# Another order for the layers of the first block of a two-block transformer kernel

## The chip, the cores and the metric

The kernel runs on one core of one Trainium2 chip. The metric is the device time of one execution in microseconds (us): three runs of the kernel before gave 2479.18, 2482.4 and 2484.06 us, median 2482.4. Everything is computed in float32, and the whole program is one launch.

## What is computed

A sequence of 256 tokens of width 1024 goes through two blocks, each with two layers. The change touches the first block alone. Each of its layers computes this (`hgrn2` is a gated linear recurrence, `nsa` an attention with three branches):

```
h = rmsnorm(x);  proj = h @ w_in            # 1024 x 7704, split in 13 parts
o_h = rmsnorm(hgrn2(hq, hf, hi)) * silu(hz) # 8 heads of 128
k_cmp, v_cmp = compress(kc), compress(vc)   # 15 blocks of 32 tokens, stride 16
for each of 8 heads in 2 groups:
    o_c = softmax(q k_cmp) v_cmp ; o_s = softmax(q ks) vs ; o_w = softmax(q kw) vw
    o_n = g0 * o_c + g1 * o_s + g2 * o_w    # g = sigmoid(ng), 24 columns
o_n = o_n * silu(nz)
x = x + rmsnorm([o_h, o_n] @ w_out)         # 2048 x 1024
```

The recurrence's state decays per channel and token by f; its lower bound is 0 in layer 0 and a learned one in layer 1, so layer 1 has a longer chain of elementwise work between the projection f and its first product. With four blocks of 64 keys and 16 blocks selected, the selected branch is full causal attention here. The second block (two feed-forward parts, a three-way mixing, a cross attention, twice) is not changed.

## The kernel before, in words

**Program.** `make_plan` (line 624 on) writes one list of steps by hand-written generators, and five functions (`tensor_program`, `scalar_program`, `vector_program`, `gpsimd_program`, `sync_program`) turn it into the queue of each engine. A step is issued on every engine in the order of the list, so each engine works through its parts of the steps in that order, and an instruction that waits holds everything behind it on its engine. The buffers come from two shelves, first in first out: 24 SBUF units of 128x1024 (`NUNIT`) and the 8 PSUM banks. Who takes one waits for the events with which it was given back.

**Matmuls.** A projection multiplies in three passes of fp32r: high x high, low x high and high x low. A weight piece (1 MB, 128x2048) is loaded by SyncE into one of 6 slots; ScalarE copies its high part (L1872, 1.9 us), VectorE subtracts for the low part (L2053, 2.3 us), and for each third piece GpSimd does it (L2540, 4.6 us). `split_next` lets this run at most three pieces (`LEAD`) ahead of the piece last finished. `mm_tok` gives a "wide" step: 12 matmuls of 512 columns (L1625, L1629, L1635), tokens in the partitions; a piece has one for each half t of the tokens. `mm_ch` gives a "channel" step: 12 matmuls of 256 columns (L1649, L1652, L1655), channels in the partitions.

**Interleaving.** `weave(plan, main, side, us)` takes one step of `main`, then steps of `side` until `us` microseconds' worth of matmul columns have been planned. `both` takes a step of each of several generators in turn. A `"rest"` from the side ends its turn early.

**A layer's order** (`first_layer`): (1) norm, keys and values of both branches; (2) the projection c, then `compress` beside q and the first part of nz with the gates; (3) `nsa(0)` and `nsa(1)` in turn, with the rest of nz, hv and hz beside them (`proj_all`); (4) `hgrn_qf(0)`, the projections f and q of head group 0 and their elementwise chain; (5) `hgrn_heads(0)` beside `hgrn_qf(1)`; (6) `hgrn_heads(1)` beside the output projection of the attention half; (7) the output projection of the recurrence half (`tail`).

**The parts.** An attention branch of one group and half (`nsa`) has three steps: scores (L1673, VectorE scales and masks them at L2109, takes the maximum at L2114; ScalarE the exponentials at L1920), transposes of the probabilities (L1681), and the product with the values (L1690). `nsa_out` then takes, on VectorE, the sums' inverse times the gate (L2273, L2275, L2278), and adds the scaled product of the branch to an SBUF accumulator (L2286 for the first branch, L2291 for the others). The gates are 24 columns at the head of the nz projection, so nz is cut in 6656+512, 7168+512 and 7680+24 columns, the last with 24-column matmuls. `hgrn_heads` has a product within the token (L1745), one across the halves (L1756), and seven levels: VectorE makes the key factor (L2373), GpSimd the query factor's exponent (L2564, 1.1 us), ScalarE the exponential (L2013), VectorE the query product (L2378), TensorE the level's matmuls (L1767, 16 records), and VectorE copies them under a mask (L2384). `level` is issued `depth` levels ahead: 1 for group 0, 2 for group 1. At the end `hgrn_v` (L1777, L1779) multiplies with the values. In `compress`, `cmp_rows` (L2254) lays out the rows for `cmp_1` (L1711). `tables()` computes constants of layer 1 and of the second block, and in layer 0 it is a third stream beside attention.

Of the kernel before, what the change touches and what calls it, by code (L numbers as in the profile page):

```python
# [11 lines left out]
ALU = mybir.AluOpType  # L12
# [23 lines left out]
NUNIT = 24  # L36
# [224 lines left out]
class Memory:  # L261
    def __init__(self, nc, ctx):
# [16 lines left out]
        self.halfs = sb("halfs", [P, 16])  # L279
        self.ropes = sb("ropes", [P, 2, 224])  # L280
# [10 lines left out]
def weave(plan, main, side, us):  # L291
# [20 lines left out]
def both(*gens):  # L312
    gens = list(gens)
    while gens:
        for g in list(gens):
            more = next(g, "end")
            if more == "end":
                gens.remove(g)
            else:
                yield more  # L320


class Plan:
# [208 lines left out]
    def pv(self, name, res, nh, of, vd, need):  # L532
        bank = self.B.take()
        self.work += 4 * nh * len(res) * vd
        self.do("pv", name=name, res=[(w3, made) for _, w3, made in res], nh=nh, of=of, vd=vd, need=need, bank=bank)
# [62 lines left out]
def tail(plan, seam, ws, mid=None, first=False):  # L598

    for t in range(2):  # L600
        for wi, (w, k0, h) in enumerate(ws):
            for pi, (kk0, p) in enumerate(w):
# [6 lines left out]
        if t == 0:  # L609
            if mid:  # L610
                mid()
            seam.turn(0)
# [11 lines left out]
def make_plan(A, m, order):  # L624
# [71 lines left out]

    def first_layer(l, seam):
# [19 lines left out]

        kT, vv = U.take(), U.take()
# [15 lines left out]
        cc = U.take()  # L734
        for q, (b, pr) in enumerate((yield from proj_ch(f"{N}.c", 5120, 512))):
            cc_made = plan.copy(f"{N}.cc{q}", [pr], cc.ap[:, q * 512:q * 512 + 512], b.ap, "dve", cc.after)
            B.give(b, cc_made)

        qT = [U.take(), U.take()]
# [14 lines left out]
        def q_side():  # L754
            k_turn()
# [13 lines left out]
            yield from nz_proj([(6656, 512)])  # L769
            q_turn(1, *qrows[1])  # L770

        def q_turn(g, qs, rt):
            q_made[g] = []
# [4 lines left out]
        kcm = U.take()  # L778
        kcs, vcs = kcm.ap[:, 0:32], kcm.ap[:, 64:320]
        kc_made = []  # L780

        def compress():
            for which in range(2):
# [6 lines left out]
                   need=[cc_made, ("gT",)], after=e.after)  # L790
# [27 lines left out]
                if which == 0:  # L818
# [10 lines left out]
                                  b.ap[:, 0:32].rearrange("p (g n) -> p g n", g=2)[:, :, 0:15], "dve", kcm.after)  # L829
                else:  # L830
                    c = plan.copy(f"{C}.vc", [("cmp_2", C)], vcs[0:15, :], b.ap[0:15, 0:256], "dve", kcm.after)
# [4 lines left out]
        gates = [st(24), st(24)]  # L836
        nz = [U.take(), U.take()]
        g_made, nz_made = [None, None], [[], []]

        def nz_proj(cols):  # L840
            for c0, n in cols:
                for t, (b, pr) in enumerate((yield from proj_tok(f"{N}.z{c0}", c0, n))):
                    o = 24 if c0 == 6656 else 0
                    if o:
                        do("gates", name=(N, t), need=pr, dst=gates[t], src=b.ap[:, 0:24])
                    d0 = c0 + o - 6680
                    s = plan.silu(f"{N}.nz{c0}{t}", [pr], nz[t].ap[:, d0:d0 + n - o], b.ap[:, o:n], nz[t].after)
                    B.give(b, s, *([("gates", N, t)] if o else []))
                    nz_made[t].append(s)
                if o:  # L850
                    for t in range(2):
                        do("gates_scaled", name=(N, t), ap=gates[t])
                        g_made[t] = ("gates_scaled", N, t)
                yield
# [1838 lines left out]
```

## Time and profile before

| | |
|---|---|
| median of three runs | 2482.4 us |
| profiled execution, its own time | 2484.2 us |
| its span, first to last instruction | 2482.4 us |
| TensorE matmuls busy | 2219.2 us, 89% of the span |
| TensorE weight loads (overlap) | 1941.7 us, 78% |
| VectorE, ScalarE, GpSimd busy | 1320.1, 1017.7, 567.4 us |
| mean granted TensorE clock | 0.948 of full speed |
| chain that ended last | PE 66%, DVE 17%, ACT 9%, issue 5%, POOL 3%, DMA 1% |
| HBM | 141 GB/s over the span |

PE is TensorE, DVE VectorE, ACT ScalarE, POOL GpSimd. In a row of windows the first number is the length, then for each engine its busy time and its instructions, then the granted clock of TensorE (1.00 is 2.4 GHz, 0.50 is 1.2 GHz, and a mean between them is a mixture), the share of the DMA engines and GB/s. Length less PE busy is TensorE's idle time. In a row of a timeline stand the start, the time from the first start to the last end, the engine, the line of the kernel, and in brackets how long the engine had been idle and what ended that. Where GpSimd and VectorE run at the same time, single rows can be longer than their operation. In a row of waits stand who waited for whom, the total, how many times, and the longest.

### The profile page before, as it was taken

What the parts mean: (1) busy time and instruction counts of PE and PEld (TensorE: products, weight loads), DVE (VectorE), ACT (ScalarE), POOL (GpSimd) and SP (SyncE); (2) the same over time, 40 slices, a digit from 0 to 9 for tenths busy, and PEclk for the clock granted to TensorE, in tenths of its full rate; (3) what the DMA queues carried; (4) which work ended last, traced back from release to release, by engine and by line L of the source; (5) the groups of instructions that cost most, each with busy time, mean ns of one, the idle gap of its engine ahead of it and who ended that gap; (6) DMA issues with size and microseconds to landing.
All of it is one profiled execution on the core that took longest, in us unless ns stands there. A gap on an engine that the chain in (4) does not pass through costs nothing.

```text
span 2482.4 us, 29939 instructions
## 1 busy us (share of the span) xinstructions
PE 2219.2 (89%) x12751; PEld 1941.7 (78%) x12751; DVE 1320.1 (53%) x1663; ACT 1017.7 (41%) x1340; POOL 567.4 (23%) x215
## 2 busy tenths in 40 slices
PE   6897888899877799988998999999998998898998
PEld 5786876678776689867877879988986777686997
DVE  4456564536576554356476554345435545755533
ACT  4244543334443344335444444334433445443442
POOL 1110222202023132222122323223222222222221
PEclk9988998999888999999999999999999999998999
DMA  7442212444122345524444436555553354343553
GB/s 234 140 141 80 103 68 88 142 156 138 66 76 78 102 170 187 176 102 136 158 165 140 158 110 204 187 178 171 187 188 109 117 169 169 127 158 105 191 186 108
DMA packets 190974, 351.63 MB, mean 142 GB/s; under 512 B 8124, under 2 KB 84984, under 8 KB 190840
## 3 DMA queue, kind: packets, MB, share of 16 engines
q1 hardware_dynamic: 189400, 344.46, 41.2%
q0 software_dynamic: 1440, 5.24, 0.6%
q8 instruction: 101, 1.65, 0.3%
q14 instruction: 33, 0.27, 0.0%
HBM read 348.63 MB, written 1.05 MB: 141 GB/s over the span
## 4 chain that ended last, share of the span: by engine, by line
PE 66%; DVE 17%; ACT 9%; issue 5%; POOL 3%; DMA 1%; SPq 0%; DVEq 0%; POOLq 0%; ACTq 0%
PE bank L1629 12%; PE bank L1635 12%; PE bank L1625 12%; PE bank L1655 7%; PE bank L1652 7%; PE bank L1649 7%; ACT high L1872 4%; DVE raw_r L2053 3%; PE bank L1673 2%; PE bank L1690 2%; POOL raw_r L2540 2%; PE bank L1711 1%; DVE units_r L2070 1%; DVE units L2384 1%; PE bank L1664 1%
## 5 line engine op out<-in xcount | busy, mean ns | idle before, releaser
L2540 POOL TENSOR_TENSOR raw_r<-raw,high 128x2048 fp32r<-128x2048 f32 (+2 forms) x104 | 482.9, 4644 | 1391.3 <-ACT high L1872 1391.3
L1625 PE MATMUL bank<-high,units_r 128*128 128x512 f32 (+2 forms) x1728 | 702.3, 407 | 48.5 <-ACT units_r L1889 21.8
L2053 DVE TENSOR_TENSOR raw_r<-raw,high 128x2048 fp32r<-128x2048 f32 x210 | 531.4, 2538 | 388.4 <-ACT high L1872 388.4
L1629 PE MATMUL bank<-high,units_r 128*128 128x512 f32 (+2 forms) x1728 | 688.6, 399 | 11.9 <-DVE units_r L2070 11.7
L1872 ACT ACTIVATE high<-raw 128x2048 fp32r<-128x2048 f32 (+1 forms) x314 | 589.9, 1892 | 235.3 <-PE bank L1635 189.7
L1635 PE MATMUL bank<-raw_r,units_r 128*128 128x512 f32 (+2 forms) x1728 | 467.4, 393 | 4.3 <-POOL raw_r L2540 4.3
L1625 PEld LDWEIGHTS bank<-high,units_r 128*128 128x128 f32 x1728 | 337.1, 195 | 120.5 <-issue 42.0
L1629 PEld LDWEIGHTS bank<-high,units_r 128*128 128x128 f32 x1728 | 337.2, 195 | 84.9 <-DVE units_r L2070 20.3
L1649 PE MATMUL bank<-units_r,high 128*128 128x256 f32 x1600 | 399.3, 285 | 0.0
L1652 PE MATMUL bank<-units_r,high 128*128 128x256 f32 x1600 | 396.9, 284 | 0.0
L1635 PEld LDWEIGHTS bank<-raw_r,units_r 128*128 128x128 f32 x1728 | 330.4, 193 | 75.2 <-POOL raw_r L2540 7.0
L1649 PEld LDWEIGHTS bank<-units_r,high 128*128 128x128 f32 x1600 | 309.1, 193 | 0.9
L1652 PEld LDWEIGHTS bank<-units_r,high 128*128 128x128 f32 x1600 | 308.9, 193 | 0.9
L1655 PE MATMUL bank<-units_r,raw_r 128*128 128x256 f32 x1600 | 235.1, 284 | 2.4 <-POOL raw_r L2540 2.2
L1655 PEld LDWEIGHTS bank<-units_r,raw_r 128*128 128x128 f32 x1600 | 211.5, 193 | 2.8 <-POOL raw_r L2540 2.4
L1920 ACT ACTIVATE units<-units,stat 128x256 f32<-128x256 f32 (+2 forms) x176 | 74.0, 422 | 201.6 <-DVE stat L2116 201.6
L2529 POOL TENSOR_TENSOR stat<-stat,halfs 128x1 f32<-128x1 f32 (+2 forms) x64 | 43.5, 679 | 453.0 <-DVE stat L2142 197.2
L2070 DVE TENSOR_TENSOR units_r<-units,units_r 128x512 fp32r<-128x512 f32 x100 | 81.7, 846 | 72.0 <-ACT units_r L1889 69.4
L1889 ACT ACTIVATE units_r<-units 128x512 fp32r<-128x512 f32 x100 | 61.3, 631 | 140.3 <-DVE units L2062 108.5
L2081 DVE SCALAR_TENSOR_TENSOR units<-units,bank 128x512 f32<-128x512 f32 (+2 forms) x68 | 43.5, 652 | 121.0 <-ACT units L1900 121.0
L1767 PE MATMUL bank<-units 128*128 128x128 f32 x448 | 66.0, 309 | 30.2 <-DVE units L2378 19.6
L1767 PEld LDWEIGHTS bank<-units 128*128 128x128 f32 x448 | 62.7, 222 | 34.1 <-ACT units L2013 15.5
(217 smaller groups left out, 1820.6 us busy)
## 6 DMA issues: line engine op xcount, KB each, us to landing
raw<-in_ffn_w_dram SPq DMA_DIRECT2D x132, 1024.0 KB, 5.1
raw<-in_w_in_dram SPq DMA_DIRECT2D x108, 1024.0 KB, 4.9
raw<-in_w_out_dram SPq DMA_DIRECT2D x24, 1024.0 KB, 5.0
raw<-in_cross_wkv_dram SPq DMA_DIRECT2D x16, 1024.0 KB, 5.0
raw<-in_w_branch_dram SPq DMA_DIRECT2D x12, 1024.0 KB, 4.8
raw<-in_cross_wq_dram SPq DMA_DIRECT2D x8, 1024.0 KB, 5.2
raw<-in_cross_wo_dram SPq DMA_DIRECT2D x8, 1024.0 KB, 4.9
raw<-in_w_in_dram SPq DMA_DIRECT2D x4, 832.0 KB, 4.3
```

What stands on the lines that cost most here:

```text
L1625: pe.matmul(o, h.high(k0 + k)[:, span], w[:, k, :], start=start and k == 0, stop=False, skip_group_check=True)
L1629: pe.matmul(o, h.low(k0 + k)[:, span], w[:, k, :], start=False, stop=False, skip_group_check=True)
L1635: product = pe.matmul(o, h.high(k0 + k)[:, span], w[:, k, :], start=False, stop=stop and k == p.k - 1, skip_group_check=True)
L1649: pe.matmul(o, w, h.high(k0 + k), start=first and k == 0 and c % 2 == 0, stop=False, skip_group_check=True)
L1652: pe.matmul(o, w, h.low(k0 + k), start=False, stop=False, skip_group_check=True)
L1655: product = pe.matmul(o, p.lo[:, k, c * P:c * P + P], h.high(k0 + k), start=False, stop=last and k == p.k - 1, skip_group_check=True)
L1767: score = pe.matmul(bank.ap[:, i * P:i * P + P], r3[:, i, t * P:t * P + P], r3[:, i, t * P:t * P + P], start=True, stop=True, skip_group_c ...
L1872: act.activation(high, p.raw, ACT.Copy).then_inc(*mark(s.whigh, ("whigh", p.i)))
L1920: done = act.activation(p3[:, h, :], p3[:, h, :], ACT.Exp, bias=mx[:, h:h + 1], scale=1.0, accum_out=sm[:, h:h + 1])
L2053: dve.tensor_tensor(low, p.raw, high.bitcast(F32), ALU.subtract).then_inc(*mark(s.wlow_v, ("wlow", p.i)))
L2070: dve.tensor_tensor(seen(lo.r, t), seen(lo.ap, t), seen(hi.r, t).bitcast(F32), ALU.subtract).then_inc(*mark(s.alow, ("low", name, q)))
L2540: pool.tensor_tensor(low, p.raw, high.bitcast(F32), ALU.subtract).then_inc(*mark(s.wlow_p, ("wlow", p.i)))
```

## The change

`first_layer` gets another order; the second block's code stays as it is.

- After keys and values, `hgrn_qf(0)` comes first. Then four streams run in turn through one `weave` with 2.0 us a step: `compress`, `nsa(0)`, `nsa(1)` and `recurrence` (both head groups, one after the other), in layer 0 with `tables()` as the fifth. A stream whose inputs aren't planned yet yields `"stuck"` and is passed over; where all are stuck, `weave` takes one step of the side.
- The side is `fill()`: all projections in one row (c, q, gates, hv and hz of group 0, then after the end of recurrence 0 f and q of group 1, nz in two halves, hv and hz of group 1), then, once attention is done, the output projection of head group 0 of the recurrence and of group 0 of attention (`out_early`). The `tail` has the two others.
- The gates have a projection of their own in channel form (24 rows), transposed back to tokens; nz is then 2 x 512 columns, and no 24-column matmul is left.
- The gate and the inverse of the sum are multiplied into the probabilities before they are transposed (`nsa_gate`), so that the three branches add up in one PSUM bank, held by the group and half from its first branch to `nsa_cat`.
- hv and hz are kept per head group; `depth` is 1 for both groups; the compressed keys and values lie in a buffer of their own; `NUNIT` is 26.

```diff
 def weave(plan, main, side, us=None):
...
+        if more == "stuck":
+            assert live and next(side, "end") != "end"
+            yield
+            continue
...
 def both(*gens):
     gens = list(gens)
     while gens:
+        went = False
         for g in list(gens):
             more = next(g, "end")
             if more == "end":
                 gens.remove(g)
-            else:
+                went = True
+            elif more != "stuck":
+                went = True
                 yield more
+        if not went:
+            yield "stuck"
...
+        def gate_proj():
+            ((_, p),) = plan.weight(w_in, 0, 8, 6656, 24)
+            b, u, b2 = B.take(), U.take(), B.take()
+            do("gate_rows", name=N, p=p, h=h, bank=b, dst=u)
...
+            do("gate_turn", name=N, src=u.ap, bank=b2, dst=both_gates)
...
         def nsa(g):
+            while q_made[g] is None or len(kc_made) < 2:
+                yield "stuck"
...
                     u, p3, sm, soft = plan.scores(S_, [*q_made[g], *k_need], 4, L, of, 1, bias, P ** -0.5)
                     yield
+                    do("nsa_gate", name=S_, need=[soft, g_made], sm=sm, ..., p3=p3, L=L, some=br > 0)
                     res = plan.turned(...)
                     yield
...
-                    b, pr = plan.pv(S_, res, 4, vf, P, [*v_made, *kc_made])
-                    do("nsa_out", ...)
+                    acc, pr = plan.pv(..., None if br == 0 else acc, br == 0, br == 2)
                     yield
+                while (g, t) not in nz_made:
+                    yield "stuck"
...
-            depth = 1 + hg
+            depth = 1
...
+            while ("v", hg) not in st_ or ("z", hg) not in st_:
+                yield "stuck"
...
+        def recurrence():
+            yield from hgrn_heads(0)
+            while ("qf", 1) not in st_:
+                yield "stuck"
+            yield from hgrn_heads(1)
+
+        def projections():
+            yield from cmp_proj()
+            k_turn()
+            yield from q_proj()
+            yield from hgrn_v(0)
+            yield from hgrn_z(0)
+            while ("done", 0) not in st_:
+                yield "rest"
+            yield from hgrn_qf(1)
+            yield from nz_proj(0)
+            yield from nz_proj(1)
+            yield from hgrn_v(1)
+            yield from hgrn_z(1)
...
+        def out_early():
+            while len(cat_made) < 4:
+                yield "rest"
+            for t in range(2):
+                turn_h(0, t)
+            yield from plan.mm_tok(f"{N}.oh0", plan.weight(w_out, 0, 4, 0, 1024), h_T[0], yb, last=False)
+            turn_n(0)
+            yield from plan.mm_tok(f"{N}.on0", plan.weight(w_out, 1024, 4, 0, 1024), n_T[0], yb, ...)
+            turn_n(1)
...
+        yield from hgrn_qf(0)
+        streams = [compress(), nsa(0), nsa(1), recurrence()] + ([tables()] if l == 0 else [])
+        yield from weave(plan, both(*streams), fill(), 2.0)
...
+        tail(plan, nxt, [(plan.weight(w_out, 1536, 4, 0, 1024), 0, n_T[1]),
+                         (plan.weight(w_out, 512, 4, 0, 1024), 0, h_T[1])],
+             before={(0, 1): lambda: turn_h(1, 0), (1, 0): lambda: turn_h(1, 1)})
...
+    def nsa_gate(name, need, sm, gsel, p3, L, some, **_):      # vector_program
+        hold.wait_ge(*at(need[0]))
+        if not some:
+            dve.tensor_scalar(sm, sm, 1e-30, None, ALU.max).then_inc(*mark(s.vstep))
+        dve.reciprocal(sm, sm).then_inc(*mark(s.vstep))
+        dve.tensor_tensor(sm, sm, gsel, ALU.mult).then_inc(*mark(s.vstep))
+        dve.tensor_tensor(p3, p3, bc(sm, L), ALU.mult).then_inc(*mark(s.vout, ("gated_p", name)))
```

## Rows read from the trace of the kernel before

**Rows 1.** Windows by stage, layer 0: length, busy by engine, PEclk, DMA, GB/s.
```profile
17.60:49.10 31.50, 27.18 (x113) 22.32 (x114) 21.18 (x18) 16.05 (x18) 9.06 (x3) 1.00 0.56 187
49.10:128.30 79.20, 67.46 (x413) 58.28 (x412) 34.49 (x65) 21.46 (x26) 11.42 (x4) 0.93 0.53 168
128.30:209.00 80.70, 80.19 (x399) 67.65 (x399) 47.17 (x99) 36.03 (x77) 13.71 (x3) 0.90 0.41 139
209.00:259.20 50.20, 35.52 (x174) 30.71 (x172) 30.26 (x91) 22.08 (x62) 2.75 (x1) 0.73 0.08 27
259.20:283.10 23.90, 23.24 (x194) 23.03 (x193) 15.09 (x17) 14.08 (x14) 5.98 (x2) 1.00 0.38 133
283.10:347.10 64.00, 48.17 (x368) 47.08 (x368) 40.43 (x54) 26.11 (x28) 19.27 (x14) 0.92 0.24 83
347.10:402.60 55.50, 46.72 (x257) 41.40 (x257) 35.11 (x49) 20.17 (x20) 11.05 (x7) 0.88 0.22 76
402.60:431.00 28.40, 24.66 (x102) 19.37 (x103) 8.97 (x16) 11.13 (x17) 7.39 (x5) 0.88 0.21 72
```

**Rows 2.** Windows by stage, layer 1, same columns.
```profile
431.00:464.30 33.30, 29.08 (x126) 22.49 (x125) 22.64 (x23) 14.88 (x21) 8.87 (x4) 0.95 0.41 133
464.30:543.00 78.70, 67.03 (x405) 57.60 (x403) 34.47 (x65) 21.46 (x26) 11.79 (x4) 0.93 0.52 168
543.00:625.90 82.90, 82.82 (x425) 70.66 (x426) 43.23 (x79) 36.46 (x88) 13.71 (x3) 0.92 0.41 140
625.90:665.60 39.70, 28.14 (x152) 24.95 (x151) 23.13 (x52) 15.83 (x43) 2.41 (x1) 0.79 0.08 27
665.60:694.60 29.00, 23.31 (x195) 23.11 (x193) 20.66 (x22) 15.96 (x16) 3.06 (x2) 0.94 0.42 145
694.60:773.90 79.30, 54.42 (x369) 52.88 (x369) 57.61 (x62) 28.28 (x30) 25.86 (x14) 0.82 0.16 54
773.90:828.70 54.80, 45.54 (x257) 40.02 (x257) 34.72 (x49) 20.12 (x20) 10.66 (x7) 0.91 0.23 77
828.70:857.20 28.50, 24.68 (x100) 19.47 (x101) 8.89 (x16) 10.93 (x17) 7.25 (x5) 0.88 0.20 66
```

**Rows 3.** Waits of TensorE, 283.1 to 347.1 us: total, times, longest.
```profile
PE bank L1767 <- DVE units L2378: 10.0, 5, 3.6
```

**Rows 4.** Window inside wide projections of layer 0.
```profile
90.10:100.90 10.80, 10.80 (x49) 8.65 (x48) 4.28 (x12) 4.59 (x5) 4.92 (x1) 1.00 0.70 190
```

**Rows 5.** Timeline, VectorE's rearranged rows of compression, and GpSimd's split.
```profile
61.51 6.14 DVE L2254 TENSOR_TENSOR units<-units,gT 128x240 f32<-128x240 f32 x4
...
61.88 4.51 POOL L2540 TENSOR_TENSOR raw_r<-raw,high 128x2048 fp32r<-128x2048 f32 x1 [11.37 <-ACT high L1872]
...
113.79 1.96 DVE L2254 TENSOR_TENSOR units<-units,gT 128x240 f32<-128x240 f32 x4
```

**Rows 6.** Window over three covered levels at depth 2.
```profile
360.40:375.70 15.30, 15.30 (x102) 13.84 (x100) 8.66 (x11) 6.51 (x6) 3.64 (x1) 1.00 0.24 73
```

**Rows 7.** Windows over the 24-column projection, both layers.
```profile
143.90:158.40 14.50, 14.50 (x62) 12.88 (x61) 4.04 (x12) 3.66 (x4) 4.53 (x1) 0.54 0.42 145
559.60:572.80 13.20, 13.20 (x62) 11.94 (x61) 4.12 (x12) 3.64 (x4) 4.52 (x1) 0.61 0.46 159
```

**Rows 8.** Groups of VectorE, 17 to 431 us, and its timeline.
```profile
L2291 DVE SCALAR_TENSOR_TENSOR units<-bank,stat,units 128x128 f32<-128x128 f32 x32 | 9.0, 344 | 9.2 <-PE bank L1690 8.8 <-DVE stat L2278 0.3
...
L2151 DVE TENSOR_TENSOR units<-units 128x1024 f32<-128x1024 f32 x1 | 1.2, 1226 | 0.0
...
178.56 4.18 DVE L2273 TENSOR_SCALAR stat<-stat 128x4 f32<-128x4 f32 x1
```

**Rows 9.** Timeline of three engines at 372 us.
```profile
372.06 5.14 POOL L2540 TENSOR_TENSOR raw_r<-raw,high 128x2048 fp32r<-128x2048 f32 x1 [23.29 <-ACT high L1872]
...
379.61 1.36 DVE L2378 TENSOR_TENSOR units<-units 128x512 f32<-128x512 f32 x1 [6.86 <-ACT units L2013]
...
381.76 0.55 PE L1767 MATMUL bank<-units 128*128 128x128 f32 x1 [3.10 <-DVE units L2384]
```

More of the change, by code:

```diff
@@ L595, in turn, with tail @@
             plan.pump()
-def tail(plan, seam, ws, mid=None, first=False):
+def tail(plan, seam, ws, first=False, before=None):
     for t in range(2):
         for wi, (w, k0, h) in enumerate(ws):
+            if before and (t, wi) in before:
+                before[t, wi]()
             for pi, (kk0, p) in enumerate(w):
@@ L609, in tail @@
         if t == 0:
-            if mid:
-                mid()
+            if before and "mid" in before:
+                before["mid"]()
             seam.turn(0)
@@ L732, in first_layer @@
             yield
[L734 to L739, printed above, removed]
+        qT = []
         q_made = [None, None]
@@ L1020, in hgrn_heads @@
             U.give(a01, ("hgrn_v", H, 1))
-            if hg == 1:
-                for t in range(2):
-                    U.give(vh[t], ("hgrn_v", H, 1))
-        def proj_all():
-            yield from nz_proj([(7168, 512), (7680, 24)])
-            yield from hgrn_proj()
-        streams = [nsa(0), nsa(1)] + ([tables()] if l == 0 else [])
-        yield from weave(plan, both(*streams), proj_all(), 1.6)
-        for u_ in (kT, vv, kcm):
-            U.give(u_, *ends)
-        U.give(accs, *cat_made[0], *cat_made[1])
@@ new lines, in first_layer @@
+        h_T, n_T = [], []
+        yb = []
+        def out_early():
+            while len(cat_made) < 4:
+                yield "rest"
+            h_T.append(plan.pairs(1))
+            for t in range(2):
+                turn_h(0, t)
+            yb.extend([[B.take(), B.take()], [B.take(), B.take()]])
+            yield from plan.mm_tok(f"{N}.oh0", plan.weight(w_out, 0, 4, 0, 1024), h_T[0], yb, last=False)
+            plan.give_pairs(h_T[0], ("prod", f"{N}.oh0", 1))
+            turn_n(0)
+            yield from plan.mm_tok(f"{N}.on0", plan.weight(w_out, 1024, 4, 0, 1024), n_T[0], yb, first=False,
+                                   last=False)
+            plan.give_pairs(n_T[0], ("prod", f"{N}.on0", 1))
+            turn_n(1)
@@ L1464, in out_proj @@
         plan.pump()
-        tail(plan, nxt, [(plan.weight(wd, 512 * q, 4, 0, 1024), 4 * q, sT) for q in range(2)], lambda: turn(1),
-             first=True)
+        tail(plan, nxt, [(plan.weight(wd, 512 * q, 4, 0, 1024), 4 * q, sT) for q in range(2)], first=True,
+             before={"mid": lambda: turn(1)})
         plan.give_pairs(sT, ("prod", name, 1))
@@ L1682, in keys, with pv @@
         turned.then_inc(*mark(s.turned, ("turnk", name, j)))
-    def pv(name, res, nh, of, vd, need, bank, **_):
+    def pv(name, res, nh, of, vd, need, bank, first, last, **_):
         for n in (*need, *bank.after):
@@ L1906, in gates, with gate_rows @@
         act.activation(dst, src, ACT.Tanh, bias=0.0, scale=0.5).then_inc(*mark(s.gate, ("gates", *name)))
+    def gate_rows(name, bank, dst, **_):
+        hold.wait_ge(*at(("gate_rows", name)))
+        for n in dst.after:
+            hold.wait_ge(*at(n))
+        act.activation(dst.ap[0:24, 0:256], bank.ap[0:24, 0:256], ACT.Tanh, bias=0.0, scale=0.5).then_inc(
+            *mark(s.gate, ("gates", name)))
     def rope(name, need, src, dst, hd, o, hf, after, **_):
```

257 lines of the change are left out of this document (137 added, 120 removed).

## The prediction

> **What bounds the kernel now.** I read the windows by stage first, then who TensorE waited for in the stages that lose, then single rows of VectorE and GpSimd. The change touches nothing behind the first block, whose last stage ends at 857 us. Its sixteen stages [rows 1, 2] take 413.4 and 426.2 us, and TensorE idles 60.3 and 71.2 us of them (length less PE busy), 131.5 us or 15.7%. The clock column adds to it. A stretch at 1.2 GHz does half the work, so (1 - clock) x length is at most what the low level costs: 42.4 us in layer 0 and 46.4 in layer 1. It is an upper bound, because part of each slow stretch is idle time anyway.
>
> The reader is to see three things in the rows. Where projections lie between the steps of attention (128.3 to 209, 543 to 625.9), idle is 0.5 and 0.1 us. Where they have run out (209 to 259.2, 625.9 to 665.6), it is 14.7 and 11.6 us at clocks of 0.73 and 0.79. And the recurrence costs 15.8 and 8.8 us of idle in layer 0, 24.9 and 9.3 in layer 1, waiting in the first of these stages 10.0 us, five times, for VectorE's query product of a level [rows 3]. So the block is bound by TensorE's order of work: how many dependent steps lie next to independent matmuls.
>
> **The change, part by part.** I count in steps. A wide projection step is 12 matmuls of 512 columns. 48 of these matmuls take 10.8 us [rows 4], so a step is 2.7 us. A channel step (12 of 256) is 1.44 us, since 192 take 23.2 us (259.2 to 283.1, rows 1).
>
> *Steps and cover.* Before, a layer's interleaved part has 5 steps of compression, 36 of attention (2 groups x 2 halves x 3 branches x 3) and 22 of recurrence. From the generators, attention has 22 covered and 14 bare, each recurrence 8 covered and 3 bare. The number of projection steps stays the same, so the new order can't cover everything either. I followed the new round robin. Recurrence 0 runs alone against the 8 channel steps of the compression input (4 steps of the stream), then against q beside compression, and finishes its levels there. Attention starts against hv0 and hz0 (8 wide steps). The two value products of recurrence 0 and some 4 attention steps are bare, because the filler says "rest" until recurrence 0 is done. f and q of group 1 (16 channel steps) follow, until both attention groups are stuck on their nz. Then 16 wide steps (nz0, nz1, hv1, hz1) lie beside recurrence 1 and attention. About 14 steps are bare at the end, in three streams until the recurrence ends, then one or two. The 8 output steps of h0 and n0, which lay beside recurrence 1, now run after all that, dense.
>
> *Idle that stays*, layer 0 / layer 1, from the rows of the stages:
> - beginning: 4.3 / 4.2, unchanged.
> - f and q of group 0 up to the first recurrence product: 0.7 (23.90 less 23.24), and as much again for the wait at that product, / 5.7 us, unchanged: the bound arithmetic of layer 1 is as exposed as now.
> - compression: 11.7 / 11.7 now, mostly the rearranged rows, one set of four operations taking 6.14 us beside a GpSimd split, the other 1.96 without [rows 5]. A transposition and one wide step now lie before the first product, but a level's VectorE work does too. Between 5 and 14, I take 9.
> - four levels beside channel steps, one level ahead: at this depth now 10.0 us in 5 waits [rows 3]; at depth 2 with wide steps none at all in 15.3 us [rows 6]. Between 0 and 8, I take 3.
> - value products and bare attention of the first half: between 2 and 8, I take 4.
> - from f of group 1 to the recurrence's next product: 0 to 8, I take 2 / 4.
> - levels and attention beside 16 wide steps: one level ahead, with some 4.8 us between products (two channel steps and the product), the chain was late by 2 us each time [rows 3], so it takes about 7 us. Two ahead it was never late [rows 6]. Now a turn has two or three wide steps and what lies between, over 7 us. Between 0 and 12, I take 3.
> - the 14 bare steps: now 14.7 / 11.6. Three streams hide more of each other, but the last branch of group 1 is alone. Between 5 and 18, I take 10.
> - early output and tail: 3.7 / 3.8 now, with one exposed turn more, 5 / 5.
>
> These make 41.7 and 47.9 us, 89.6 in all. Idle saved is 131.5 - 89.6 = 41.9 us.
>
> *Clock.* With the gate projection taken out (next item) the bound on the low level is 88.8 - 11.8 = 77 us for 131.5 us of idle, 0.59 per us. The other bound is 0. I take 0.4, between the two, since slow stretches hold idle time and matmuls in about equal parts (209 to 259.2: 14.7 idle, at most 2 x 13.6 slow). 41.9 x 0.4 = 16.8 us.
>
> *Gates.* The 24-column projection (48 matmuls with full weight loads) and 12 wide ones fill 14.5 and 13.2 us at clocks of 0.54 and 0.61 [rows 7]. Less 2.7 us each that is 22.3 us. The channel form has 24 matmuls of 256 columns (2.9 us) and two small transposes (0.4), 6.6 us for both layers. The clock stood at 1.00 through 192 channel matmuls in a row (259.2 to 283.1, rows 1), so I take it that it won't fall there: 15.7 us saved. If the clock falls elsewhere instead, some 4 us.
>
> *Summing in PSUM.* Per branch, VectorE loses four accumulations of 0.34 us [rows 8], and gains one product over the probabilities: 1.23 us for 1024 columns (the row of that size, rows 8), half for 512. That is within 2 us per group, off the path where covered. But the product now stands before the transposes: 0.9 to 1.6 us more per bare branch, against which VectorE no longer waits for the branch's product before the other group's work. I cost it at nothing (-4 to +8). Two banks are held over three branches; six are left for streams that take one or two at a time: nothing, at most 3 us. The two extra buffers and the DMAs cost nothing (the depth is priced with the levels): the same weight pieces go through the same six slots, and DMA is at 0.2 to 0.5 in these stages.
>
> *Tables.* Layer 0's table work moves from attention to the start, with its loads of activation tables in the recurrence's exponentials: 0 to 10, I take 5 us.
>
> Sum: -41.9 - 16.8 - 15.7 + 5 = -69.4 us. The profiled execution took 2484.2 us (span 2482.4), so 2414.8. It is 1.8 us above the median of the runs, so 2413.
>
> *A rule that speaks against it.* During the GpSimd split at 61.88 us one set of row operations took 6.14 instead of 1.96 us, and a VectorE operation on 4 columns took 4.18 us [rows 5, 8]. So VectorE operations with SBUF operands stand still while a split runs, and the accumulations out of PSUM do not (0.34 us each). The Trainium skill (SBUF — State Buffer, "Who interferes with whom") says that a VectorE instruction with two SBUF inputs contends with a GpSimd one that reads SBUF, and the loser blocks fully. The trace agrees. By that rule the new product over the probabilities contends, where the accumulation that it replaces did not.
>
> **The rivals.**
> - *The port decides.* A split of 4.5 us [rows 5] comes once in three pieces of 5.4 us, 28% of the covered time, so it meets some 3.4 of 12 gate products a layer, 4.2 us each: 28 us in two layers if nothing hides them. 2441. For: each is on the path to the transposes. Against: the small operation before it was held as well (4.18 us) and TensorE idled 0.5 us in that stage. Chance 0.12.
> - *Cover is moved, not added.* The recurrence keeps much of its 58.8 us of idle beside attention, and 20 us of idle go: 20 x 1.4 + 15.7 - 5 = 39, so 2445. For: the count of bare steps hardly changes. Against: interleaved streams need cover less. Chance 0.20.
> - *Streams hide each other better.* 60 us of idle go: 60 x 1.4 + 15.7 = 100, so 2384. Chance 0.13.
> - *Slower: a blocked level holds everybody.* One level ahead, VectorE waits in its queue for the exponential. Where a GpSimd split of 5.14 us stood before the level's GpSimd part, VectorE waited 6.86 us and TensorE 3.1 us [rows 9]. Now attention's scores and the weight splits are queued behind that wait. If all 28 levels cost 3.1 us of idle, that is 28 x 3.1 x 1.4 = 122 us where the recurrence loses 58.8 x 1.4 = 82 now: 40 more, less 15.7: 2507. It decides from 2.5 us per level. Against: only each third split is GpSimd's. Chance 0.07.
> - *It doesn't overlap as it says*, because streams are stuck on each other and the fillers run alone: within 0.2% of now (2482), chance 0.03.
>
> **How the numbers follow.** My forecast, 2413, has 0.45. About 0.2% (5 us) is what a measurement of this kernel can tell from no change. Faster: 0.45 + 0.12 + 0.20 + 0.13 = 0.90. Same 0.03, slower 0.07. The forecast's own costs add up to some 25 us either way; the range from 2382 to 2460 takes in the three faster rivals, and leaves the ends of the clock's and the levels' bounds and the slower ones out.
>
> **What would show it.** Right: the two layers end some 70 us earlier than 876; the 24-column matmuls are gone and no slow stretch stands in their place; the idle before the level products beside wide steps is under 1 us each; a bare stretch of 25 to 40 us before the output projection. Wrong: long waits of VectorE for level exponentials with scores queued behind; the gate product taking 4 us again and again with TensorE idle; or the bare stretch over 50 us a layer.

## The result: 1.8% slower, and the profile after

The changed kernel took 2527.27 us (median of 4 runs, 2522.65 to 2533.7), beside 2482.82 us before: a ratio of 1.0183, with a 95% interval of 1.0157 to 1.0209. The forecast was 2413, so the time lies 114 us from it and on the other side.

The page after: the span, the busy times, the clock by slices, the chain that ended last, and the one group of instructions that is new near its top.

```profile
span 2523.5 us, 29681 instructions
...
PE 2209.0 (88%) x12707; PEld 1926.6 (76%) x12707; DVE 1294.9 (51%) x1593; ACT 1019.5 (40%) x1334; POOL 567.9 (23%) x215
...
PEclk9988888999888899998999999999999999898999
...
PE 65%; DVE 17%; ACT 9%; issue 4%; POOL 3%; DMA 1%; SPq 0%; POOLq 0%; ACTq 0%; DVEq 0%
...
L1741 PE MATMUL bank<-consts,units 128*128 128x128 f32 (+1 forms) x232 | 44.2, 343 | 113.1 <-DVE units L2375 107.1
```

TensorE is busy 10 us less than before (2209.0 after 2219.2), and the 232 transposes of L1741 had 113.1 us of idle time in front of them, 107.1 us of it waiting for VectorE's L2375. Over the first block, from 17.6 us to its end (857.2 before, 898.3 after), the windows of the kernel before (which sum up [rows 1, 2]) and of the changed one are these, with the length and then busy time (count) of TensorE, its weight loads, VectorE, ScalarE and GpSimd, the clock, the DMA share and GB/s:

```profile
17.60:857.20 839.60, 708.16 (x4028) 621.03 (x4029) 478.04 (x767) 331.02 (x519) 164.24 (x71) 0.89 0.33 109
```

```profile
17.60:898.30 880.70, 692.33 (x3973) 600.78 (x3972) 452.78 (x696) 332.38 (x513) 165.41 (x71) 0.90 0.32 104
```

Idle (length less PE busy) went from 131.4 to 188.4 us, at about the same clock. Who TensorE waited for in these windows, with the total, the number and the longest, first before, then after:

```profile
PE bank L1767 <- DVE units L2378: 19.6, 10, 3.6
PE bank L1711 <- DVE units L2254: 18.6, 4, 7.1
PE bank L1681 <- ACT units L1920: 17.8, 10, 2.9
PE bank L1779 <- DVE units L2384: 14.5, 3, 9.4
PE bank L1767 <- DVE units L2384: 10.5, 5, 3.1
```

```profile
PE bank L1741 <- DVE units L2375: 107.1, 20, 12.7
PE bank L1771 <- DVE units L2347: 17.9, 4, 8.5
...
PE bank L1831 <- ACT units L1981: 10.3, 3, 5.7
PE bank L1842 <- DVE units L2460: 10.0, 2, 6.2
...
PE bank L1853 <- DVE units L2460: 5.6, 2, 3.2
```

The levels of the recurrence (L1767 before, L1853 after), which waited 19.6 + 10.5 us (10.0 of it in the one stage of [rows 3]), wait 5.6 us. This is what the new order was to bring. Compression's first products (L1711 before, L1771 after) wait as they did, 18.6 and 17.9 us. The recurrence's first product (L1831, L1745 before) waits 10.3 us, after 16.6 in two rows that the block leaves out; its product across the halves (L1842, L1756 before) has 10.0 us, of which it had 2.1 before. But the transposes of the probabilities (L1681 before, L1741 after), which waited 17.8 us for ScalarE's exponentials, now wait 107.1 us, 20 times, for the product of gate and probabilities on VectorE. That one line is more than the whole difference.

The longest of these waits, in the timeline of the changed kernel on all engines. L1733 are the scores, L2013 their exponentials, L1865 the recurrence's value product, L2146 a weight split, L2202 and L2207 the scores' scaling and maximum, L2174 a silu, L2221 to L2472 the recurrence's output norm, L2375 the gate product, L1741 the transposes:

```profile
208.84 1.05 PE L1733 MATMUL bank<-units 128*128 128x128 f32 x8
...
209.42 0.18 ACT L2013 ACTIVATION_READ_ACCUMULATOR units<-units,stat 128x1 f32 x1
...
209.73 1.06 PE L1865 MATMUL bank<-units 128*128 128x128 f32 x8
211.44 2.29 DVE L2146 TENSOR_TENSOR raw_r<-raw,high 128x2048 fp32r<-128x2048 f32 x1 [3.52 <-ACT high L1958]
213.65 0.68 DVE L2202 SCALAR_TENSOR_TENSOR units<-bank,consts 128x512 f32<-128x512 f32 x1
214.37 0.69 DVE L2207 TENSOR_REDUCE stat<-units 128x4 f32<-128x512 f32 x1
...
216.85 1.05 ACT L1986 ACTIVATE units<-bank 128x512 f32<-128x512 f32 x2
217.45 1.28 DVE L2174 SCALAR_TENSOR_TENSOR units<-units,bank 128x512 f32<-128x512 f32 x2 [2.19 <-ACT units L1986]
...
218.66 0.68 DVE L2221 TENSOR_REDUCE stat<-units 128x4 f32<-128x512 f32 x1
...
219.62 1.02 POOL L2611 TENSOR_TENSOR stat<-stat,halfs 128x4 f32<-128x4 f32 x1 [17.53 <-DVE stat L2223]
220.66 0.69 DVE L2472 TENSOR_TENSOR units<-units,stat 128x512 f32<-128x512 f32 x1 [1.13 <-POOL stat L2611]
...
222.71 0.69 DVE L2375 TENSOR_TENSOR units<-units,stat 128x512 f32<-128x512 f32 x1
...
223.46 1.12 PE L1741 MATMUL bank<-consts,units 128*128 128x128 f32 x4 [12.67 <-DVE units L2375]
```

The reader is to see what stands between the exponentials of the first group, done at 209.6 us, and its gate product at 222.7. VectorE works in the order of the list, and in this list the gate product is issued with the transposes. Ahead of it stand a split, the other group's scores and maximum, two silu, and the recurrence's norm, which itself goes to ScalarE and to GpSimd and back. Some small table operations stand there too, which the block leaves out. The product takes 0.69 us; what it waited behind takes 11.3, from 211.44 on, and before that VectorE itself stood for 3.52 us, until ScalarE had made the high part of the weight piece. TensorE's own queue is in order too, so it stands still for 12.67 us with all other streams' matmuls behind the transposes.

### The profile page after: what moved, and what is told of

It is laid out like the page before. It is cut to its first block, busy times and chain, and to the rows that moved or that the text cites. A ratio compares the mean times of both kernels' runs of the same rounds, so it can differ in the third digit from the quotient of the medians.

```text
span 2523.5 us, 29681 instructions
## 1 busy us (share of the span) xinstructions
PE 2209.0 (88%) x12707; PEld 1926.6 (76%) x12707; DVE 1294.9 (51%) x1593; ACT 1019.5 (40%) x1334; POOL 567.9 (23%) x215
## 4 chain that ended last, share of the span: by engine, by line
PE 65%; DVE 17%; ACT 9%; issue 4%; POOL 3%; DMA 1%; SPq 0%; POOLq 0%; ACTq 0%; DVEq 0%
PE bank L1689 11%; PE bank L1685 11%; PE bank L1695 11%; PE bank L1715 7%; PE bank L1709 7%; PE bank L1712 7%; ACT high L1958 4%; DVE raw_r L2146 3%; PE bank L1750 2%; PE bank L1733 2%; POOL raw_r L2622 2%; ACT units L2013 2%; PE bank L1741 1%; PE bank L1771 1%; PE bank L1724 1%
## 5 line engine op out<-in xcount | busy, mean ns | idle before, releaser
L2146 DVE TENSOR_TENSOR raw_r<-raw,high 128x2048 fp32r<-128x2048 f32 x210 | 535.0, 2555 | 415.3 <-ACT high L1958 415.3
L1685 PE MATMUL bank<-high,units_r 128*128 128x512 f32 (+1 forms) x1696 | 697.7, 411 | 52.3 <-ACT units_r L1975 24.6
L1689 PE MATMUL bank<-high,units_r 128*128 128x512 f32 (+1 forms) x1696 | 682.7, 403 | 12.7 <-DVE units_r L2163 12.6
L1695 PE MATMUL bank<-raw_r,units_r 128*128 128x512 f32 (+1 forms) x1696 | 459.7, 393 | 2.1 <-POOL raw_r L2622 2.1
L1685 PEld LDWEIGHTS bank<-high,units_r 128*128 128x128 f32 x1696 | 331.3, 195 | 127.5 <-issue 47.8
L1689 PEld LDWEIGHTS bank<-high,units_r 128*128 128x128 f32 x1696 | 330.9, 195 | 88.0 <-DVE units_r L2163 23.0
L1695 PEld LDWEIGHTS bank<-raw_r,units_r 128*128 128x128 f32 x1696 | 323.9, 191 | 72.6 <-POOL raw_r L2622 3.9
L2013 ACT ACTIVATE units<-units,stat 128x256 f32<-128x256 f32 (+2 forms) x176 | 74.1, 422 | 212.2 <-DVE stat L2209 212.2
L1741 PE MATMUL bank<-consts,units 128*128 128x128 f32 (+1 forms) x232 | 44.2, 343 | 113.1 <-DVE units L2375 107.1
L1741 PEld LDWEIGHTS bank<-consts,units 128*128 128x128 f32 (+1 forms) x232 | 32.7, 167 | 124.0 <-DVE units L2375 114.8
L2106 ACT ACTIVATE units<-units 128x1024 f32<-128x1024 f32 x32 | 33.9, 1058 | 166.9 <-DVE units L2455 111.3
```

Source lines behind the costliest of these rows:

```text
L1685: pe.matmul(o, h.high(k0 + k)[:, span], w[:, k, :], start=start and k == 0, stop=False, skip_group_check=True)
L1689: pe.matmul(o, h.low(k0 + k)[:, span], w[:, k, :], start=False, stop=False, skip_group_check=True)
L1695: product = pe.matmul(o, h.high(k0 + k)[:, span], w[:, k, :], start=False, stop=stop and k == p.k - 1, skip_group_check=True)
L1741: turned = pe.transpose(bank.ap[0:rows_, i * P:i * P + P], p3[:, i, j * P:j * P + rows_], ident)
L2013: done = act.activation(p3[:, h, :], p3[:, h, :], ACT.Exp, bias=mx[:, h:h + 1], scale=1.0, accum_out=sm[:, h:h + 1])
L2146: dve.tensor_tensor(low, p.raw, high.bitcast(F32), ALU.subtract).then_inc(*mark(s.wlow_v, ("wlow", p.i)))
```

## Experiments

Each kernel was timed in three rounds beside the kernel before on the same chip. The ratios are to those runs. Theory A: the gate product stands in front of the transposes on a VectorE queue that others fill. Theory B: the four interleaved streams are what costs, and the transposes only show it.

### The two halves of the change apart

**e1_out_back**, the new order without the sum in PSUM:

```diff
-                    do("nsa_gate", name=S_, need=[soft, g_made], ...)
-                    res = plan.turned(..., [("gated_p", S_)], ...)
+                    res = plan.turned(..., [soft], ...)
...
-                    acc, pr = plan.pv(..., None if br == 0 else acc, br == 0, br == 2)
+                    b, pr = plan.pv(S_, res, 4, vf, P, [*v_made, *kc_made])
+                    do("nsa_out", ..., bank=b, acc=acc, first=br == 0, old=old, after=[plan.gp_used] ...)
```

> The changed kernel with the attention's old end: the transposes wait for the exponentials alone, each branch has its own PSUM bank, and VectorE scales and adds the branch's output in SBUF (1024 columns that lie idle then, the post-norm gain's). The new order of layers, the channel-form gates and the depth of 1 stay. Theory A (the gate product ahead of the transposes puts VectorE's queue on TensorE's path, 107 us of idle at the transposes in two layers): idle there falls to the 15 to 25 us of before, so 85 us go, with the clock 2415 to 2440 us. Theory B (the interleaving of four streams on an in-order VectorE is what costs, and the transposes only show it): the idle moves to the value products, the levels and the output sums, 2490 to 2525 us.

Measured: 2455.57 us, ratio 0.9891 (0.9874 to 0.9907), 71.7 us faster than the changed kernel and 26.5 faster than before. A holds: B had the time at 2490 or more. It is also 15 us above A's range, on which more below. Its window over the first block and its waits (L1746 are the transposes, L1776 the first product of compression, L1785 the turn behind it, L1858 the levels, L1870 the recurrence's value product):

```profile
17.60:828.60 811.00, 680.32 (x3994) 592.26 (x3994) 473.30 (x762) 332.25 (x513) 165.25 (x71) 0.93 0.34 114
```

```profile
PE bank L1746 <- ACT units L2018: 31.5, 9, 5.9
PE bank L1776 <- DVE units L2352: 19.4, 4, 8.5
...
PE bank L1870 <- DVE units L2483: 10.5, 2, 5.2
...
PE bank L1785 <- DVE units L2483: 9.5, 2, 4.8
PE bank L1858 <- DVE units L2477: 5.5, 2, 3.0
```

**e2_psum_only**, the other half: the kernel before, with `nsa_gate` ahead of the transposes and `pv` into one bank.

> The kernel before with one part of the change: gate and inverse sum multiplied into the probabilities ahead of the transposes, the branches summed in PSUM; its own order of layers and the rest as before. Theory A: the transposes wait for VectorE here too, 2 to 4 us in each of 24 branch pairs and groups, 2530 to 2570 us. Theory B: VectorE has attention alone beside the weight splits here, so little is lost: 2475 to 2495 us.

Measured: 2543.43 us, ratio 1.0249 (1.0233 to 1.0264). The sum in PSUM costs 61 us in the old order, where neither the recurrence nor compression lies beside attention, and 72 in the new one. Theory B had this run at 2475 to 2495 and is out: this half alone makes the kernel slower than the whole change does. The transposes' wait there, 70.9 us of it:

```profile
PE bank L1675 <- DVE units L2275: 70.9, 18, 6.7
```

### Place in the queue, or length of the work

**e3_gate_early** moves one line of the changed kernel:

```diff
+                    do("nsa_gate", name=S_, need=[soft, g_made], ...)
                     yield
-                    do("nsa_gate", name=S_, need=[soft, g_made], ...)
                     res = plan.turned(S_, u, p3, 4, ..., [("gated_p", S_)], ...)
```

> The changed kernel with the gate product issued in the scores' step, so ahead of the step of projection and of the other streams in VectorE's queue, instead of together with the transposes. Nothing else differs. Theory A1 (what stands before the gate product in VectorE's queue decides: other scores, splits, the recurrence's output): half or more of the 107 us goes, 2440 to 2480 us. Theory A2 (the length of the chain exponential, three small operations and product decides): VectorE now stands still for the exponentials, and the time stays within 2505 to 2540 us.

Measured: 2466.02 us, ratio 0.9942 (0.9927 to 0.9957), 61 us faster than the changed kernel with the same instructions. The timeline of the same place in this kernel, and the transposes' total wait:

```profile
199.34 1.05 PE L1733 MATMUL bank<-units 128*128 128x128 f32 x8
...
200.43 0.69 DVE L2202 SCALAR_TENSOR_TENSOR units<-bank,consts 128x512 f32<-128x512 f32 x1 [4.62 <-PE bank L1733]
...
204.18 0.69 DVE L2375 TENSOR_TENSOR units<-units,stat 128x512 f32<-128x512 f32 x1
...
204.93 0.66 PE L1741 MATMUL bank<-consts,units 128*128 128x128 f32 x4
205.57 2.29 DVE L2146 TENSOR_TENSOR raw_r<-raw,high 128x2048 fp32r<-128x2048 f32 x1 [0.70 <-ACT high L1958]
...
211.51 0.69 DVE L2375 TENSOR_TENSOR units<-units,stat 128x512 f32<-128x512 f32 x1
...
212.26 1.12 PE L1741 MATMUL bank<-consts,units 128*128 128x128 f32 x4 [6.68 <-DVE units L2375]
```

```profile
PE bank L1741 <- DVE units L2375: 39.0, 9, 6.7
```

The first group's gate product now begins at 204.2 us, 3.8 us after its scores were scaled and ahead of the split, and its transposes follow at 204.9. The second group's transposes still wait 6.68 us, behind a split that stood before the scores. In the changed kernel both groups' transposes came together, from 223.5 us on.

**e4_no_product** takes the product out and leaves its three small operations where they were; the branches stay unscaled.

```diff
-        dve.tensor_tensor(sm, sm, gsel, ALU.mult).then_inc(*mark(s.vstep))
-        hold.wait_ge(*last(s.vstep))
-        dve.tensor_tensor(p3, p3, bc(sm, L), ALU.mult).then_inc(*mark(s.vout, ("gated_p", name)))
+        dve.tensor_tensor(sm, sm, gsel, ALU.mult).then_inc(*mark(s.vout, ("gated_p", name)))
```

> The changed kernel without the product over the probabilities (0.1 to 1.2 us on VectorE in each branch): the branches come out unscaled, so this part of the computation is left out; the three small operations stay at their place, and the transposes wait for them. If the place in the queue decides (A1): 24 products of 0.8 us on average go, 2495 to 2510 us, and 80 us or more of idle stay at the transposes. If the product itself decides (held by GpSimd's splits, 4 us at a time): 2440 to 2470 us.

Measured: 2515.83 us, ratio 1.0134 (1.0119 to 1.0149), 11 us less than the changed kernel. That is 6 us above the range for A1, which had named the idle at the transposes rightly, and 46 above that of its rival. The transposes still wait 93.6 us, now for an operation on 4 columns:

```profile
PE bank L1741 <- DVE stat L2373: 93.6, 20, 11.9
```

So the place costs 61 us and the work itself some 11. The two counts meet: e3 is 10.5 us above e1, which has the place and the work of before. Those 10.5 us also hold whatever the PSUM banks cost that are kept over three branches. No run has that cost by itself; since the product alone is 11, it is small.

**e10_psum_early** does the same move in `e2_psum_only`.

> e2_psum_only (the order of before, gate and inverse sum into the probabilities, sum in PSUM) with the gate product issued in the scores' step, ahead of the side's step. e2_psum_only was 61 us slower than before. If the place in VectorE's queue decides in the old order too, most of this goes: 2485 to 2505 us. If there the bare branches' longer chain decides: 2520 to 2540 us.

Measured: 2501.03 us, ratio 1.0081 (1.0066 to 1.0096). 42 of the 61 us go with the place, in the upper part of the range for the queue, and 20 stay, twice as much as in the new order. The transposes' wait for the product falls from 70.9 to 37.4 us.

### What the new order and the gates bring

**e5_gates_only**: the kernel before with `gate_rows` and `gate_turn`, and nz in two projections of 512 columns.

> The kernel before with the gates' channel form alone: 24 matmuls of 256 columns and two small transposes in place of the 24 columns at the head of nz, and nz in two projections of 512 columns; order, attention and recurrence as before. By the prediction's term: 15.7 us less, 2464 to 2470 us, the stretch at 1.2 GHz behind the 24-column matmuls gone. Rival: the clock falls somewhere else nearby, and only the matmuls' own 4 to 6 us are left, 2475 to 2479 us.

Measured: 2482.89 us, ratio 0.9994 (0.9982 to 1.0006): nothing. Neither expectation holds. The stretch at 1.2 GHz is gone (clock 0.99, the first row). Over the block (second row) TensorE is busy 12.2 us less than before, and idle 142.6 us in place of 131.4: what the matmuls gave back, a wait took. The 24-column steps had been cover as well. Without them the first scores (L1682) come earlier and wait 6.18 us for the compressed values. The copy of these (L2119) takes 0.41 us; it stood in VectorE's queue behind a weight split (L2095), which waited for ScalarE's high part.

```profile
143.00:160.00 17.00, 17.00 (x88) 13.58 (x87) 8.04 (x18) 8.80 (x16) 4.60 (x1) 0.99 0.38 124
17.60:856.20 838.60, 696.00 (x3988) 607.19 (x3987) 477.59 (x761) 331.96 (x513) 172.07 (x71) 0.90 0.33 109
```

```profile
134.24 2.29 DVE L2095 TENSOR_TENSOR raw_r<-raw,high 128x2048 fp32r<-128x2048 f32 x1 [4.17 <-ACT high L1907]
136.45 0.41 DVE L2119 COPY units<-bank 15x256 f32<-15x256 f32 x1
136.91 1.89 PE L1682 MATMUL bank<-units 128*128 128x15 f32 x8 [6.18 <-DVE units L2119]
```

There are two such waits, one a layer, 12.1 us together.

**e16_gates_24col** asks the same in the new order: `e1_out_back` with the gates in token form (`proj_tok(f"{N}.g", 6656, 24)`).

> e1_out_back with the gates as 48 matmuls of 24 columns in token form again (in one projection of their own, at the place of the channel form). e5_gates_only moved the old order by nothing, because the first scores then waited for the compressed values. If the channel form pays in the new order (matmul time and clock): 5 to 9 us slower in each layer's start, 2465 to 2473 us. If it is worth nothing here either: within 4 us of 2455.

Measured: 2470.18 us, ratio 0.9956 (0.9941 to 0.9970), 14.6 us above e1, as the first expectation had it. Here the channel form is worth what it was to be: TensorE is busy 694.8 us in the block with the 24-column form and 680.3 without, and idle 130.4 and 130.7, so no wait takes its place.

```profile
17.60:842.80 825.20, 694.83 (x4036) 605.22 (x4035) 468.82 (x762) 332.89 (x515) 165.04 (x71) 0.92 0.34 112
```

**e6_rows_step** lets other steps in between the rearranged rows and their product: one `yield` after `cmp_rows`.

> As e1_out_back, and compression gives its turn away between the rearranged rows and the product that needs them, so that one more projection step lies in between. TensorE waited 19.4 us for the rows in four places in e1_out_back. If those waits were on the path: 10 to 16 us less than e1_out_back, 2440 to 2447 us. If each covering step is only taken from a bare step further on: within 5 us of it, 2450 to 2460 us.

Measured: 2444.93 us, ratio 0.9851 (0.9836 to 0.9866), 10.6 us below e1, within the first expectation: the wait was on the path. Of the products' 19.4 us of wait 0.9 are left; 10.9 of them come back at the first scores, which wait 12.1 us for the compressed keys and values (1.2 in e1).

**e7_early_output** lets the output projection of the first head group go before attention is planned:

```diff
         def out_early():
-            while len(cat_made) < 4:
-                yield "rest"
             h_T.append(plan.pairs(1))
...
+            while (0, 1) not in cat_made:
+                yield "rest"
             turn_n(0)
...
+            while len(cat_made) < 4:
+                yield "rest"
             turn_n(1)
```

> As e1_out_back, and the output projection of the recurrence's first head group (4 wide steps) no longer rests until all of attention is planned; it lies beside the last steps of attention and recurrence 1, and that of attention's first group follows as soon as its own results are planned. If the bare steps at the end cost what cover can hide (about 8 us of idle at the transposes a layer, and the clock): 10 to 25 us less, 2430 to 2446 us. If they take what they take because VectorE and ScalarE are the bound there: 2450 to 2458 us.

Measured: 2465.19 us, ratio 0.9930 (0.9914 to 0.9946), 10 us slower than e1, which neither expectation had. The covering step needs an operand of its own, and that comes late: the first matmuls wait for the high part (ScalarE) and the low part (VectorE) of the turned rows, behind what these engines have queued for the streams. In two layers the waits of L1692 for ScalarE are 25.5 us, where e1 has 10.7 at the same line.

```profile
325.23 0.77 PE L1692 MATMUL bank<-high,units_r 128*128 128x512 f32 x1 [7.50 <-ACT units_r L1982]
328.27 0.79 PE L1696 MATMUL bank<-high,units_r 128*128 128x512 f32 x1 [2.27 <-DVE units_r L2170]
```

**e9_no_rests** has e6, e7, and no rest before f and q of the second head group; **e13_rows_norest** the same without e7.

```diff
             yield from hgrn_z(0)
-            while ("done", 0) not in st_:
-                yield "rest"
             yield from hgrn_qf(1)
```

> Both of these, and also no rest between hz0 and the projections f and q of the recurrence's second group, so that no step of any stream is bare while a projection is left. If cover is what matters, the sum of the parts and some 5 to 10 us more, 2415 to 2435 us; if cover only moves, within 10 us of e1_out_back.

> e9_no_rests without the early output: e1_out_back, a step between the rearranged rows and their product, and no rest before f and q of the second head group. e7_early_output was 10 us slower than e1_out_back, since the projection's operands came late behind full queues. If that price is the same here: 2425 to 2435 us. If the early output paid in e9_no_rests: 2440 to 2450 us.

Measured: e9 2440.02 us, ratio 0.9833 (0.9818 to 0.9847), which lies between its two expectations; e13 2423.63 us, ratio 0.9766 (0.9747 to 0.9785), 1.4 us below the range for an early output that costs as much as in e7. It costs 16 us here. Taking out the rest brings 21 us over e6. e13 is the fastest of all, 57.7 us below the kernel before. Its first block:

```profile
17.60:799.40 781.80, 669.88 (x3975) 584.83 (x3974) 463.00 (x760) 331.20 (x512) 163.38 (x71) 0.93 0.35 117
```

**e14_depth2** is e13 with `depth = 1 + hg`.

> e13_rows_norest with the recurrence's second head group two levels ahead, as before the change. The levels wait 5 us in all at depth 1 in e1_out_back, so within 4 us of e13_rows_norest if the streams beside hide the chain; 8 us or more slower if the longer wait of VectorE's queue holds attention.

Measured: 2429.28 us, ratio 0.9792 (0.9776 to 0.9808), 5.6 us above e13, between the two expectations and with intervals that touch. The idle time of the block is the same (111.6 and 111.9 us). A second level ahead brings nothing in the new order; whether it costs is not settled.

## Why the prediction was wrong

**The step that failed** is "Summing in PSUM": "I cost it at nothing (-4 to +8)". It measured +71.7 us (changed kernel against e1), +61.4 in the old order. I had seen both facts that decide it. The product "now stands before the transposes", and VectorE waits in its queue. But I added up the product's duration and not the place of the instruction. The old transposes waited for ScalarE's exponentials; of VectorE's queue only what stood ahead of the scores' maximum mattered to them. The new dependency puts everything that VectorE has queued between the scores and the transposes on TensorE's path: one projection step (2.7 us, [rows 4]) lies between them, and the 20 waits were 5.4 us on average and up to 12.7. I wrote "off the path where covered". But of the 20 waits 14, with 70.2 of the 107.1 us, began within 5 us behind a projection matmul: cover brings its own splits to the same VectorE queue (in nine of the 14 VectorE ran a weight split, 2.29 us, or a part of one while TensorE waited). The six in bare steps were 6.1 us each. With this term right, the sum would have been 2413 + 72 = 2485, no change.

**The sum of the rest was -69.4; it measured -26.5** (e1 against before):
- *Gates*: -15.7 forecast from [rows 7], -14.6 in the new order (e16), 0 in the old (e5). Right in the new order, and by luck: the prediction did not ask what lies beside the gates, which decided it in the old one.
- *Levels*: idle of 30.1 us before, 5.5 in e1 and 5.6 after. I had 3 + 3 a layer kept, 12 in all. Better than forecast, and depth 1 was no loss (e14).
- *Clock*: with the gates' part, the bound (1 - clock) x length fell from 92.4 to 56.8 us in e1, 35.6, where the clock's two decimals leave some 4 us open at each end. I had 16.8, and 11.8 in the gates. The size is about right and the reason is not: the idle time that was to bring the 16.8 stayed.
- *Tables*: +5 forecast. The block has 12 loads of activation tables of 1.28 us each before and 12 after, so no load was added; no run has the rest of the term by itself.
- *Idle*: 41.9 us were to go. Measured: 131.4 before and 130.7 in e1, so nothing. The levels gave back 24.6 us and the value products 4.0 (14.5 to 10.5). It came again elsewhere: 31.5 us at the transposes (17.8 before), 19.4 in compression's products (18.6 before) and 9.5 at the turn behind them, and 9.7 at the product across the halves, which hardly waited before. I took each stream's wait as if cover alone decided. But the streams meet in VectorE's queue and at the PSUM banks. In e1 compression's turn at 165.21 us had its own operand at 152.3; it waited 4.79 us for a bank that a level's mask (L2483) gave back, and the mask stood on VectorE behind a weight split. In the old order the turn never met a level. e6 and e13 show how much was only a matter of places in the list: with one more step between and one rest fewer, idle is 111.9 us, busy time 10 us less, and the time 31.9 us less than e1's.

**The rivals.** The port did not decide: the rival had some seven products in two layers meet a GpSimd split, and none of the 24 did. They took at most 1.226 us; the small operation of [rows 8] had taken 4.18. (In the block the columns are the shortest, median and longest duration in ns, the first and last start, and the shapes; the longest is the 1.23 us that I had taken for 1024 columns.)

```profile
L2375 DVE TENSOR_TENSOR units<-units,stat x24: 220/693/1226, 187.1 to 836.4; 128x60 f32<-128x60 f32 x8, 128x512 f32<-128x512 f32 x8, 128x1024 f32<-128x1024 f32 x8
```

The rule of the Trainium skill that I cited (SBUF — State Buffer, "Who interferes with whom") agreed with the trace before; of this product the trace shows nothing for or against it, since none of the 24 ran while GpSimd was at work. In one of the 20 waits (5.79 us, up to 787.3) an operation ahead of the product, the key factor of a level, took 3.49 us beside a GpSimd split, where its median is 0.68. Otherwise the time went in the queue. "A blocked level holds everybody" had the right side and the wrong place: the levels waited 5.6 us in all, and of the 107.1 us at the transposes VectorE stood some 6 us, in four of the waits, for a level's exponential. It was the general case of it that came true, a wait in one engine's in-order queue which holds another stream. "Cover is moved, not added" (2445) is nearest to what the order does by itself (2455).

**What I said would show it.** "the idle before the level products beside wide steps is under 1 us each": right; the two waits that there are, 5.6 us together, stand beside channel steps. "long waits of VectorE for level exponentials", a sign of being wrong: 50.4 us in 32 waits after 47.4 in 32, so hardly more than before. No slow stretch in the place of the 24 columns: right. The two layers end some 70 us earlier: wrong, 41 us later at the same point (898.3 after 857.2). "a bare stretch of 25 to 40 us before the output projection": it was 53 us in each layer (350.6 to 403.8 and 792.5 to 846.1 without a projection matmul), my mark for wrong, and TensorE idled in it:

```profile
348.00:405.00 57.00, 36.16 (x202) 32.14 (x201) 26.59 (x42) 15.96 (x40) 2.02 (x2) 0.78 0.05 19
790.00:846.00 56.00, 35.40 (x195) 31.74 (x193) 26.07 (x41) 13.87 (x36) 2.02 (x2) 0.76 0.05 19
```

20.8 and 20.6 us idle where I had 10, at clocks of 0.78 and 0.76.

## What to carry to other kernels

When an operation moves from behind a matmul to in front of one, price it by what its engine has queued at that place, not by its duration: here 0.7 us of work cost TensorE 5.4 us on average in each of 20 places, and moving one line up by one step gave back 61 of 72 us with the same instructions. Interleaved streams that share an in-order engine also share its waits, so list for each new dependency what stands before it there. And cover is worth something only if its own operands are ready in time: those of the projections of f and q, whose input is made at the start of the layer, were (e13), those of the output projection were not (e7).

## What was not expected of the hardware

The granted clock was 0.54 and 0.61 in the windows of the 24-column matmuls [rows 7], mostly the level of 1.2 GHz, and stood at 0.99 where they had been replaced by 24 matmuls of 256 columns (e5), and yet the time didn't change: 12.2 us of matmul time went and 11.2 us of idle came. Here matmuls at the low clock, beside a chain that had to be waited for anyway, cost nothing. In the new order the same replacement was worth 14.6 us (e16). And with the same idle time, e1 ran at a clock of 0.93 over the block against 0.89, and almost all of its gain is busy time: 708.2 us of matmuls became 680.3. Of these 27.8 us the gates are 14.5 (e16 against e1). The other 13.3 go with a higher clock elsewhere in the block (0.92 in e16, gates as before); why it is granted with the same idle time is not shown.
